# Mixture-of-experts products on Trainium2: 64-token stationaries split into 32-token column groups, and pairs for visits of three groups

## The chip, the cores and the metric

One core of one Trainium2 chip runs the whole kernel. The metric is the device time of one execution in microseconds (us); the figure compared is the median of several runs. A profiled execution has a span, measured by the hardware profiler, and a device time of its own a little above it. All data are float32.

## What is computed

One encoder layer: a mixer (attention and a state-space branch, about the first quarter of the time, not touched by the change), and then a mixture of experts over 512 tokens with 32 experts, four of which each token uses:

```python
logits = t @ w_router + b_router
top_val, top_idx = lax.top_k(logits, TOP_K)
top_w = softmax(top_val)
...
def expert_block(xb, e):
    g = xb @ w_gate[e] + b_gate[e]
    u = xb @ w_up[e] + b_up[e]
    g = minimum(g, 7.0)
    u = clip(u, -7.0, 7.0)
    act = g * sigmoid(1.702 * g) * (u + 1.0)
    return act @ w_down[e] + b_down[e]
...
out = zeros_like(t).at[row_tok].add(ys * row_w[:, None])
```

Each of `w_gate[e]`, `w_up[e]`, `w_down[e]` is 1024 x 1024 float32, 4 MB. The 96 matrices, some 400 MB, must all be read from memory once.

## The kernel before

**Positions, groups and visits.** Experts are ranked by their number of tokens, and processed one at a time at 32 positions. The table `RANK_GROUPS` (line 56) says how many groups of `TOK` = 32 tokens a rank gets, and `positions()` mixes large and small experts so that the work up to a position stays near `PACE` = 2.65 groups per position. The result, in order of position, is 3 3 2 3 2 3 3 2 3 3 2 3 2 3 2 2 4 2 2 4 2 2 4 2 2 2 5 2 1 5 1 1 groups, 82 in all. A position is served by one visit, a position of five groups by two, one of four groups and one of one. So there are 15 visits of two groups, 9 of three, 5 of four and 5 of one.

**The product.** For each visit and each of three matrices `product()` (line 1991) goes through eight blocks k of 128 rows of the matrix. The activations, transposed so that the contraction lies on the partitions, are the stationary operand; the weights stream. A group of 32 tokens that goes alone ("a single") has four matmuls for each k: the same 128x32 stationary is loaded in column group q = 0..3 of the array, and streams the q-th quarter of the weight's columns, 256 of them. Its result lies on 32 partitions for each quarter. Two groups that go together ("a pair") have two matmuls for each k: a 128x64 stationary in each half of the array, and each streams 512 columns. `pairs(vi)` and `singles(vi)` (lines 554 and 557) decide: a visit with an even number of groups is all pairs, one with an odd number all singles. `part_columns(vi)` (line 560) lists the parts with their columns in the accumulator. I call all matmuls of a part for one k a **round**. The trace has two records for each float32 matmul, so a round of a pair has four records and a round of a single has eight.

**The weights.** The weights come in 384 pieces of 1 MB (two blocks k each), issued by SyncE (SP) in the fixed order `STREAM` through a ring of `NRING` = 17 buffers. SP may issue the load of piece n only when the product that read piece n - 17 has released its buffer (`load` and `piece_used`, the issue itself is line 699). 17 pieces are there, or on their way, when the first product starts.

**Around the products.** PE's order is written out by hand (`stage` and the two tables of hooks in the block of TensorE): within the gate and up products of position j it makes the token lists of position j + 2 (line 1942, and `replicate`, line 1954), turns the tokens' rows of position j + 1 (line 1970) and turns the activations of position j - 1 (line 1983). VectorE (DVE) adds the bias to each product (`plus_bias`, the operation itself is recorded at line 1154), clamps and multiplies (lines 1518, 1532, 1534), and copies the expert's bias rows out to all groups (`biases`, a stream shuffle at line 1546). ScalarE (ACT) weighs the rows of the down product (line 1111). GpSimd (POOL) adds them to the output with accumulating indirect DMAs, one for each part (`scatter`, line 855): a single writes quarter rows of 1 KB, a pair half rows of 2 KB. It also gathers the tokens' rows (line 843). All DMAs of SP and POOL share 16 DMA engines.

Of the kernel before, what the change touches and what calls it, by code (L numbers as in the profile page):

```python
# [17 lines left out]
KT = DM // P  # L18
# [27 lines left out]
TOK = 32  # L46
# [44 lines left out]
VISITS, AT = visits()  # L91
NV = len(VISITS)
# [206 lines left out]
def hybrid_layer(nc, d, out, hn):  # L299
    ctx = ExitStack()  # L300
    with ctx:
# [28 lines left out]
        gm_c = const[:, C_GM:C_EPS]  # L330
# [87 lines left out]
        pieces = [cut(slots[n], KP, DE) for n in RING_AT]  # L418
# [130 lines left out]
        at_turn = {u: divmod(n, 2) for n, u in enumerate(TURNING)}  # L549
        at_unit = {u: divmod(n, SETS) for n, u in enumerate(UNITS)}  # L550
        at_piece = {u: divmod(n, NRING) for n, u in enumerate(STREAM)}
        scattered = [sum(g if (g := VISITS[w][1]) % 2 else g // 2 for w in range(v)) for v in range(NV + 1)]

        def pairs(vi):
            return 0 if vi.j is None or vi.G % 2 else vi.G // 2

        def singles(vi):
            return vi.G - 2 * pairs(vi)
# [584 lines left out]
        def _(dve):  # L1143
            v = nc.vector
# [321 lines left out]
            def index(vi):  # L1466

                c = spread(vi)
                use = vi.turns["d", 0]
                ps = wait_turned(dve, use)  # L1470
                at_least(dve, s_gath[vi.b], vi.gathers * 16)
                v.tensor_scalar(out=index_of(vi)[0:c, :].bitcast(I32), in0=ps[0:c, 0:1], scalar1=far_c[0:c, vi.G - 1:vi.G], scalar2=None,  # L1472
                                op0=ALU.add).then_inc(s_idx, 1)
                if pairs(vi) == 1 and not singles(vi):
                    ins = v.tensor_copy(dmask[vi.b][0:c, 0, :], ps[0:c, 0:2])
                else:
                    n = pairs(vi) + singles(vi)
                    blocks = {(0, 4): gm_c[:, 2:6], (2, 0): gm_c[:, 0:2], (0, 3): gm_c[:, 2:5],
                              (0, 1): gm_c[:, 2:3]}[pairs(vi), singles(vi)]
                    ins = v.tensor_tensor(out=dmask[vi.b][0:c, 0:n, :],  # L1480
                                          in0=ps[0:c, 0:2].unsqueeze(1).to_broadcast([c, n, 2]),
                                          in1=blocks[0:c, :].unsqueeze(2).to_broadcast([c, n, 2]), op=ALU.mult)
                ins.then_inc(s_tfree[use[1]], 1)
# [200 lines left out]
        def _(pe):  # L1684
# [301 lines left out]
            def product(vi, m, piece, first, last_visit, hooks=None):  # L1986
# [14 lines left out]
                for r in range(PIECES):  # L2001
                    pturn, slot = piece(m, r)
                    if first:
                        pe.wait_ge(s_raw[slot], 16 * (pturn + 1))
                    for kk in range(KP):
                        k = r * KP + kk
                        if hooks and k in hooks:
                            hooks[k]()
                        for n_, col, w in part_columns(vi):
                            t0, tn = col * TOK // QW, w * TOK // QW  # L2010
                            if m < 2:
                                x = xT[:, k, t0:t0 + tn]
                            else:
                                x = aT[n_][:, r % 2 * KP + kk, r // 2, :] if w == HW else aT[n_][:, kk, r, :]
                            for q in range(DM // w):
                                last = T.matmul(ps[q * tn:(q + 1) * tn, col:col + w], x,  # L2016
                                                pieces[slot][:, kk, q * w:(q + 1) * w],
                                                start=(k == 0 and col % 512 == 0), stop=(k == KT - 1),
                                                skip_group_check=True)
                    if last_visit and r < PIECES - 1:  # L2020
                        last.then_inc(s_used[slot], 1)
                last.then_inc(s_ufull[n], 1)
# [107 lines left out]
```

## Time and profile before

| | us |
|---|---|
| median of 3 runs | 1365.55 (1364.6 to 1369.87) |
| the profiled execution, its own time | 1366.18 |
| its span | 1364.3 |
| PE busy in the span | 1307.2 |
| DVE busy | 484.7 |
| ACT busy | 212.6 |
| POOL busy | 170.3 |

The expert products run from 353 us to 1358 us of the span. The profile records matmuls with modelled ends, so a matmul's mean duration contains the depth of the pipeline; the rate of a stream of matmuls is read from the time between the first starts of two neighbouring rows of the timeline, divided by the number of records. The share of a DMA queue is the time that its packets took, over 16 engines and the stretch.

### The profile page before, as it was taken

The numbers are of one execution on the slowest core, as the hardware profiler recorded it, in microseconds if no ns is written. First come the engines' busy times: TensorE is split into PE (matmuls) and PEld (weight loads), VectorE is DVE, ScalarE is ACT, GpSimd is POOL, SyncE is SP. The second block draws the span as 40 slices with busy tenths as digits, with TensorE's granted clock in tenths as the row PEclk, the third lists the DMA queues.
The fourth block names the chain that finished last, engine by engine and source line by source line (L and its number), as shares of the span: only waits on it lengthen the run. The fifth ranks groups of instructions, "written<-read, shape, count | busy, mean of one in ns | idle before, by whom it ended". The sixth has DMA issues, their size and how long they took to land.

```text
span 1364.3 us, 25613 instructions
## 1 busy us (share of the span) xinstructions
PE 1307.2 (96%) x10758; PEld 640.4 (47%) x10758; DVE 484.7 (36%) x1124; ACT 212.6 (16%) x461; POOL 170.3 (12%) x130
## 2 busy tenths in 40 slices
PE   8999989998899999999999998999999998999995
PEld 3465565655554555555464543333333333344342
DVE  1874576645332322222223322332322322232221
ACT  2132244332101110111100110111110001001010
POOL 0031220000201111110110111010010010011001
PEclk9989999998799999999999999999999999999998
DMA  9300420044999999999999999999999999999996
GB/s 372 124 1 0 166 100 1 33 184 170 349 342 394 406 414 397 418 399 412 407 410 415 408 416 406 416 413 410 417 406 418 417 405 417 414 414 397 410 415 229
DMA packets 77925, 448.28 MB, mean 329 GB/s; under 512 B 13080, under 2 KB 16392, under 8 KB 28656
## 3 DMA queue, kind: packets, MB, share of 16 engines
q1 hardware_dynamic: 63936, 426.51, 76.2%
q0 software_dynamic: 13296, 17.98, 5.5%
q8 instruction: 88, 1.44, 0.4%
q10 hardware_dynamic: 576, 2.10, 0.4%
q14 instruction: 29, 0.24, 0.0%
HBM read 442.61 MB, written 14.94 MB: 335 GB/s over the span
## 4 chain that ended last, share of the span: by engine, by line
PE 57%; SPq 29%; DVE 5%; DMA 5%; issue 2%; ACT 1%; POOL 1%; POOLq 0%; ACTq 0%; DVEq 0%
PE pair L2016 35%; SPq L699 28%; PE pair L1844 4%; PE pair L1745 4%; PE pair L1706 3%; DMA ring<-in_w_down 2%; DMA ring<-in_w_gate 2%; DVE rest L1154 2%; PE pair L1970 2%; PE pair L1701 2%; DVE rest L1185 1%; PE pair L1942 1%; PE pair L1983 1%; PE pair L1874 1%; PE pair L1834 1%
## 5 line engine op out<-in xcount | busy, mean ns | idle before, releaser
L2016 PE MATMUL pair<-ring,rest 128*32 128x256 f32 (+1 forms) x7952 | 832.8, 443 | 21.8 <-DMA ring<-in_w_down 14.9
L2016 PEld LDWEIGHTS pair<-ring,rest 128*32 128x32 f32 (+1 forms) x7952 | 332.4, 118 | 437.9 <-issue 288.2
L1154 DVE TENSOR_TENSOR rest<-pair,rest 128x512 f32<-128x512 f32 (+3 forms) x133 | 100.0, 755 | 426.4 <-PE pair L2016 399.0
L855 POOL DMA_INDIRECT out<-rest x57 | 89.6, 1572 | 745.1 <-ACT rest L1111 639.6
L1111 ACT ACTIVATE rest<-rest 128x256 f32<-128x256 f32 (+1 forms) x57 | 31.8, 596 | 513.6 <-DVE rest L1154 513.6
L1093 ACT ACTIVATE rest<-rest 128x512 f32<-128x512 f32 (+3 forms) x34 | 24.4, 718 | 303.4 <-DVE rest L1518 303.4
L1472 DVE TENSOR_SCALAR rest<-pair,rest 96x1 int32<-96x1 f32 (+2 forms) x34 | 7.3, 215 | 176.7 <-PE pair L1942 169.9
L1745 PE MATMUL pair<-ring 128*128 128x512 f32 (+1 forms) x192 | 69.6, 522 | 0.0
L1154 DVE TENSOR_TENSOR rest<-rest 128x512 f32<-128x512 f32 (+8 forms) x85 | 56.6, 678 | 32.1 <-ACT rest L1093 26.7
L1706 PE MATMUL pair<-ring 128*128 128x512 f32 x128 | 58.5, 617 | 5.6 <-DMA ring<-in_w_in 5.6
L2016 PE MATMUL pair<-rest 128*32 128x256 f32 (+1 forms) x592 | 62.1, 439 | 1.5 <-DMA rest<-in_w_down 1.5
L1546 DVE STREAM_SHUFFLE rest<-rest 128x512 f32<-128x512 f32 (+2 forms) x96 | 61.6, 642 | 0.0
L1844 PE MATMUL pair<-ring,rest 128*128 128x512 f32 x128 | 60.4, 621 | 0.9 <-DVE rest L1154 0.9
L843 POOL DMA_INDIRECT rest<-normed_rows,rest x34 | 35.9, 1056 | 161.7 <-DVE rest L1472 99.5
L1745 PEld LDWEIGHTS pair<-ring 128*128 128x128 f32 x192 | 36.6, 192 | 32.2 <-issue 30.7
L1970 PEld LDWEIGHTS pair<-rest 96*128 96x128 f32 (+2 forms) x272 | 35.4, 214 | 24.6 <-issue 24.6
L1970 PE MATMUL pair<-rest 96*128 96x96 f32 (+2 forms) x272 | 40.8, 293 | 3.4 <-DMA rest<-normed_rows,rest 2.7
L1706 PEld LDWEIGHTS pair<-ring 128*128 128x128 f32 x128 | 25.1, 198 | 37.3 <-issue 31.7
L1494 DVE TENSOR_SCALAR rest<-pair,rest 128x1 int32<-128x1 f32 (+2 forms) x34 | 7.5, 219 | 97.8 <-PE pair L1954 97.7
L1085 ACT ACTIVATE rest<-pair 128x256 f32<-128x256 f32 (+3 forms) x68 | 28.0, 428 | 74.6 <-PE pair L1970 73.3
L2016 PEld LDWEIGHTS pair<-rest 128*32 128x32 f32 (+1 forms) x592 | 23.7, 117 | 31.1 <-issue 17.9
L1844 PEld LDWEIGHTS pair<-ring,rest 128*128 128x128 f32 x128 | 24.2, 196 | 27.4 <-issue 26.2
(190 smaller groups left out, 860.4 us busy)
## 6 DMA issues: line engine op xcount, KB each, us to landing
ring<-in_w_gate SPq DMA_DIRECT2D x121, 1024.0 KB, 26.6
ring<-in_w_down SPq DMA_DIRECT2D x121, 1024.0 KB, 27.5
ring<-in_w_up SPq DMA_DIRECT2D x119, 1024.0 KB, 26.6
rest<-in_w_up SPq DMA_DIRECT2D x9, 1024.0 KB, 23.5
rest<-in_w_gate SPq DMA_DIRECT2D x7, 1024.0 KB, 26.5
rest<-in_w_down SPq DMA_DIRECT2D x7, 1024.0 KB, 28.1
ring<-in_w_in SPq DMA_DIRECT2D x8, 520.0 KB, 8.3
ring<-in_x SPq DMA_DIRECT2D x8, 512.0 KB, 13.0
```

What stands on the lines that cost most here:

```text
L699: sp.dma_start(pieces[slot], piece_source(m, e, r)).then_inc(s_raw[slot], 16)
L843: p.indirect_dma_start(out=hrow[vi.b][0:c, :], out_offset=None, in_=hn_d, in_offset=bass.IndirectOffsetOnAxis(ap=index_of(vi)[0:c, :].bitc ...
L855: p.indirect_dma_start(out=out_halves if w == HW else out_rows, out_offset=bass.IndirectOffsetOnAxis(ap=sidx[vi.ring][:, n:n + 1].bitcast( ...
L1085: nc.scalar.activation(rows_, src, ACT.Copy).then_inc(s_tfree[use[1]], 1)
L1111: ins = nc.scalar.activation(y, y, ACT.Copy, scale=wv[vi.ring][:, n:n + 1])
L1154: return v.tensor_tensor(out=out, in0=a, in1=b, op=op)
L1546: lk(v.stream_shuffle(out=bias_x[:, lo:hi], in_=btab[:, 3 * m * QW + lo:3 * m * QW + hi], mask=[j] * TOK))
L1706: return T.matmul(ps[:, :], w_in[:, k, XBC0 + ch * P:XBC0 + (ch + 1) * P], hTm[:, k, :], start=(k == 0), stop=(k == KT - 1))
L1745: last = T.matmul(ps[:, 0:b - a], src[:, k, t * P:(t + 1) * P], w[:, k, a:b], start=(k == 0), stop=(k == KT - 1))
L1844: last = T.matmul(ps[:, :], src[:, k, :], w[:, k, h * 512:h * 512 + 512], start=(k == 0), stop=(k == KT // 2 - 1))
L1970: last = T.transpose(ps[:, k * c:(k + 1) * c], kp_rows(hrow[vi.b][0:c, :], PIECES)[:, r, :, kk], ident[0:c, 0:c])
L2016: last = T.matmul(ps[q * tn:(q + 1) * tn, col:col + w], x, pieces[slot][:, kk, q * w:(q + 1) * w], start=(k == 0 and col % 512 == 0), stop ...
```

## The change

It does two things. In `product()` each matmul of a pair is cut in two along its tokens: a round of a pair is now four matmuls, each with a 128x32 stationary in one of four column groups, and each streams 512 columns as before; two of them stream the same half. And `pairs(vi)` is now G // 2 also for an odd G, so a visit of three groups is a pair and a single, and a visit of one stays a single. The number of scatters and the block masks follow. The overflow visits (experts with more tokens than their groups hold) keep their singles.

```diff
@@ block of positions and visits
-        scattered = [sum(g if (g := VISITS[w][1]) % 2 else g // 2 for w in range(v)) for v in range(NV + 1)]
+        scattered = [sum((VISITS[w][1] + 1) // 2 for w in range(v)) for v in range(NV + 1)]

         def pairs(vi):
-            return 0 if vi.j is None or vi.G % 2 else vi.G // 2
+            return 0 if vi.j is None else vi.G // 2
@@ index, on DVE
-                    blocks = {(0, 4): gm_c[:, 2:6], (2, 0): gm_c[:, 0:2], (0, 3): gm_c[:, 2:5],
+                    blocks = {(0, 4): gm_c[:, 2:6], (2, 0): gm_c[:, 0:2], (1, 1): gm_c[:, 0:5:4],
                               (0, 1): gm_c[:, 2:3]}[pairs(vi), singles(vi)]
@@ product, on PE
                             for q in range(DM // w):
-                                last = T.matmul(ps[q * tn:(q + 1) * tn, col:col + w], x,
-                                                pieces[slot][:, kk, q * w:(q + 1) * w],
-                                                start=(k == 0 and col % 512 == 0), stop=(k == KT - 1),
-                                                skip_group_check=True)
+                                for t in range(0, tn, TOK):
+                                    last = T.matmul(ps[q * tn + t:q * tn + t + TOK, col:col + w], x[:, t:t + TOK],
+                                                    pieces[slot][:, kk, q * w:(q + 1) * w],
+                                                    start=(k == 0 and col % 512 == 0), stop=(k == KT - 1),
+                                                    skip_group_check=True)
```

**How instructions move.** First PE, before, from the last rounds of the up product of position 1 (a visit of three, 32x256) through the gate product of position 2 (a visit of two, 64x512). The number after x counts matmuls of one kind in a row; `ring` and `rest` hold the weights and the activations, `pair` is the accumulator, and a width is that of the stationary, then the columns streamed.

```order
 L2016 MATMUL pair<-ring,rest 32x256 x120
 L2016 MATMUL pair<-ring,rest 64x512 x2
 L1983 MATMUL pair<-rest 128x128 x6
 L2016 MATMUL pair<-ring,rest 64x512 x2
 L2016 MATMUL pair<-rest 64x512 x4
 L2016 MATMUL pair<-ring,rest 64x512 x2
 L1942 MATMUL pair<-rest 96x2 x4
 L2016 MATMUL pair<-ring,rest 64x512 x12
 L1970 MATMUL pair<-rest 128x96 x8
```

The same place in the change:

```order
 L2017 MATMUL pair<-ring,rest 32x512 x4
 L2017 MATMUL pair<-ring,rest 32x256 x4
 L2017 MATMUL pair<-ring,rest 32x512 x4
 L1983 MATMUL pair<-rest 128x128 x6
 L2017 MATMUL pair<-ring,rest 32x512 x4
 L2017 MATMUL pair<-rest 32x512 x8
 L2017 MATMUL pair<-ring,rest 32x512 x4
 L1942 MATMUL pair<-rest 96x2 x4
 L2017 MATMUL pair<-ring,rest 32x512 x24
 L1970 MATMUL pair<-rest 128x96 x8
 L2017 MATMUL pair<-ring,rest 32x512 x12
 L1954 MATMUL pair<-rest 128x2
```

A visit of three now changes between four matmuls of 512 columns and four of 256 in each round. The visit of two has its hooks (lines 1983, 1942, 1970, 1954) after the same rounds, with twice as many matmuls between them.

DVE at position 0, around its up product, before (`places` of position 2, the bias add at line 1154, the clamp and the product with the gate, and the shuffle of the gate bias of the next position):

```order
 L1494 TENSOR_SCALAR rest<-pair,rest 128x1
 L1496 COPY rest<-pair 128x1
 L1154 TENSOR_TENSOR rest<-pair,rest 128x768
 L1532 TENSOR_SCALAR rest<-rest 128x768
 L1534 SCALAR_TENSOR_TENSOR rest<-rest 128x768
 L1546 STREAM_SHUFFLE rest<-rest 128x256
```

and in the change:

```order
 L1494 TENSOR_SCALAR rest<-pair,rest 128x1
 L1496 COPY rest<-pair 128x1
 L1154 TENSOR_TENSOR rest<-pair,rest 128x512
 L1154 TENSOR_TENSOR rest<-pair,rest 128x256
 L1532 TENSOR_SCALAR rest<-rest 128x768
 L1534 SCALAR_TENSOR_TENSOR rest<-rest 128x768
 L1546 STREAM_SHUFFLE rest<-rest 128x768
```

The bias add of the visit of three became two, one for the pair and one for the single, and the shuffle copies 768 columns where it copied 256.

POOL, the scatters of positions 0 and 1 between the gathers:

```order
 L843 DMA rest<-normed_rows,rest 128x1024 x3
-L855 DMA out<-rest 2048x256 x3
+L855 DMA out<-rest 1024x512
+L855 DMA out<-rest 2048x256
 L843 DMA rest<-normed_rows,rest 128x1024
```

Three scatters of quarter rows became one of half rows and one of quarter rows; nothing changed its place.

## Rows read from the trace of the kernel before

**Rows 1.** The page: DMA queues, their packets, MB, share of 16 engines.

```profile
q1 hardware_dynamic: 63936, 426.51, 76.2%
q8 instruction: 88, 1.44, 0.4%
```

**Rows 2.** Windows: busy us (x records) of each engine, PE clock, DMA share, GB/s.

```profile
353.00:400.00 47.00, 45.45 (x722) 27.38 (x726) 16.79 (x64) 5.66 (x10) 5.12 (x6) 0.97 0.94 353
400.00:500.00 100.00, 100.00 (x1236) 50.91 (x1232) 27.56 (x73) 10.13 (x21) 14.21 (x10) 1.00 1.02 399
500.00:600.00 100.00, 100.00 (x1422) 54.60 (x1418) 26.57 (x69) 11.19 (x24) 14.18 (x10) 1.00 1.02 409
1000.00:1100.00 100.00, 98.66 (x480) 36.19 (x478) 27.69 (x71) 9.88 (x17) 9.48 (x7) 1.00 1.02 413
```

**Rows 3.** DMA view, window 500 to 600: SP's queue; gate loads, us to landing.

```profile
q1 hardware_dynamic: 5336, 38.87, 93.7%
ring<-in_w_gate SPq DMA_DIRECT2D x12, 1024.0 KB, 18.6
```

**Rows 4.** The same views for 353 to 400 and 700 to 800.

```profile
q1 hardware_dynamic: 2025, 14.76, 82.7%
ring<-in_w_gate SPq DMA_DIRECT2D x3, 1024.0 KB, 6.5
...
ring<-in_w_gate SPq DMA_DIRECT2D x12, 1024.0 KB, 28.2
```

**Rows 5.** Chain that ended last, its end: start us, us, what.

```profile
1328.10 29.05 DMA ring<-in_w_down
1357.20 1.11 PE pair L2016 x16
```

**Rows 6.** Groups of PE by shape: xcount | busy us, mean ns | idle before.

```profile
L2016 PE MATMUL pair<-ring,rest 128*64 128x512 f32 x2256 | 509.4, 597 | 11.6 <-DMA ring<-in_w_down 6.4 <-DMA ring<-in_w_gate 3.6 <-DMA ring<-in_w_up 1.5
L2016 PE MATMUL pair<-ring,rest 128*32 128x256 f32 x5696 | 325.2, 382 | 10.2 <-DMA ring<-in_w_down 8.5 <-ACT rest L1103 1.1 <-issue 0.6
L1706 PE MATMUL pair<-ring 128*128 128x512 f32 x128 | 58.5, 617 | 5.6 <-DMA ring<-in_w_in 5.6
L1954 PE MATMUL pair<-rest 96*128 96x2 f32 x36 | 6.9, 262 | 0.0
```

**Rows 7.** PE's timeline, a visit of three: start us, us, what.

```profile
505.70 5.39 PE L2016 MATMUL pair<-ring,rest 128*32 128x256 f32 x96
511.02 0.84 PE L1942 MATMUL pair<-rest 128*96 128x2 f32 x8
```

**Rows 8.** PE's timeline, a visit of two.

```profile
729.41 5.37 PE L2016 MATMUL pair<-ring,rest 128*64 128x512 f32 x24
734.71 1.20 PE L1970 MATMUL pair<-rest 96*128 96x96 f32 x8
```

**Rows 9.** Line 2016's weight loads, 540 to 560: ns min/median/max.

```profile
L2016 PEld LDWEIGHTS pair<-ring,rest x276: 106/110/110, 540.1 to 560.0; 128*32 128x32 f32 x138
```

**Rows 10.** Queue of POOL in 572 to 580, then in 537 to 545.

```profile
q0 software_dynamic: 89, 0.09, 7.0%
...
q0 software_dynamic: 108, 0.20, 13.8%
```

**Rows 11.** Groups of DVE by shape, 420 to 1364.

```profile
L1546 DVE STREAM_SHUFFLE rest<-rest 128x256 f32<-128x256 f32 x31 | 13.8, 444 | 0.0
L1154 DVE TENSOR_TENSOR rest<-pair,rest 128x512 f32<-128x512 f32 x45 | 31.1, 692 | 132.1 <-PE pair L2016 132.1
L1154 DVE TENSOR_TENSOR rest<-pair,rest 128x768 f32<-128x768 f32 x22 | 21.1, 958 | 109.0 <-PE pair L2016 109.0
L1154 DVE TENSOR_TENSOR rest<-pair,rest 128x256 f32<-128x256 f32 x15 | 6.4, 425 | 40.5 <-PE pair L2016 40.4
L1546 DVE STREAM_SHUFFLE rest<-rest 128x768 f32<-128x768 f32 x6 | 6.1, 1019 | 0.0
```

**Rows 12.** PE's timeline at the turn of position 0's activations.

```profile
383.01 0.98 PE L1983 MATMUL pair<-rest 128*128 128x128 f32 x6 [1.38 <-DVE rest L1534]
```

## Prediction

> **What bounds the kernel now.** I read the page's queues first. SP's queue moved 426.5 MB and was busy for 76% of the whole span [rows 1]; nearly all of that is the 384 pieces of weights, which lie in the second three quarters. So the windows come next [rows 2]. PE looks full in each of them, but its ends are modelled, so that alone decides nothing. The DMA share is 1.02 in every window from 400 us on, at 409 to 413 GB/s, and below that only at the start: 0.94 at 353 GB/s from 353 to 400, 399 GB/s from 400 to 500. The DMA view tells why [rows 3, 4]. A piece landed 6.5 us after its issue at the start, after 18.6 us from 500 to 600, after 28.2 us from 700 to 800. SP issues a load when PE has released its buffer. With 38.87 MB in 100 us a piece of 1.05 MB takes 2.70 us of the engines, so 2 loads were on their way at the start, 7 later, 10 in the end. At the start PE's releases set the pace; from about 450 us on a queue stands before the DMA engines, and it grows: PE releases faster than they deliver. The end of the chain agrees: the last piece was issued at 1328.10, took 29.05 us, and only one piece's work and the last scatter follow it [rows 5].
>
> So the experts' phase is bound by the DMA engines except in its first 50 to 100 us. An edit counts if it takes work from the DMA engines, or lets PE release the first buffers sooner. PE's lead over DMA is small, though: the landing time grew by 9.6 us over 200 us, and a position of 12 pieces takes 12 x 2.70 = 32.4 us, so PE gains 1.55 us per position. A change that cost PE more than this would turn the bound round.
>
> **Term 1, the rounds of pairs.** I take the rates from the timeline. A single's round has 8 records: 96 records from 505.70 to 511.02 [rows 7] are 55.4 ns each, 443 ns for a group. A pair's round has 4 records: 24 from 729.41 to 734.71 [rows 8] are 220.8 ns each, 883 ns for two groups, 442 for one. The two forms cost the same per group. A full-width matmul of 512 columns takes 58.5 / 128 = 457 ns per record [rows 6]. The mean durations of 512 and 256 columns differ by 597 - 382 = 215 ns [rows 6], so streaming 512 columns takes some 430 ns in its column group. What is left per record is 457 - 430 = 27 ns for 128 tokens, 220.8 - 215 = 5.8 for 64, and 55.4 - 53.8 = 1.6 for 32.
>
> The new form, 32 tokens and 512 columns, is in no row. Its ideal is 430 / 4 = 107.5 ns per record. The nearest row by stationary and by number of groups is the single, so I take 107.5 + 1.6 = 109.1, a round of 8 records 873 ns. The ends are 107.5 (860 ns) and, with the remainder of the 64-token form, 113.3 (906 ns). Against 883 this saves 10 ns, or saves 23, or costs 23. For a visit of three the round goes from 3 x 443 = 1329 to 873 + 443 = 1316. A position has 24 rounds: -0.24 us for two groups, -0.31 for three. The visit of three also has a second small matmul pair for its index lists, 0.26 us (line 1954) [rows 6], which leaves -0.05. Where DMA is the bound this gives nothing. In the 3 or 4 positions before the queue stands it gives about **-0.4 us**, within -2 and +2 (four positions with the ends above).
>
> **Term 2, the scatters.** POOL's queue in 572 to 580, under the scatters of a visit of three, had 89 packets of 0.09 MB, thus of 1 KB: 7.0% of 8 us x 16 engines is 8.96 us, 101 ns each. In 537 to 545, under a visit of two, 108 packets of some 1.9 KB took 17.7 us, 164 ns each [rows 10]. Two packets of 1 KB that become one of 2 KB save 2 x 101 - 164 = 38 ns. A pair has 64 tokens, two half rows each: at most 128 merges per visit. The third group of a visit holds the expert's last tokens and often isn't full, and padding isn't written. The table of slots puts it in the pair, so between 64 and 128 merges happen. Nine visits: 576 to 1152 merges, 22 to 44 us of one engine, 1.4 to 2.7 us of sixteen. I take **-2.0 us**, in full, because the DMA engines are the bound there. The ends: nothing, if the freed time falls on engines that wait for others; and -7.3 us, if a 2 KB packet cost no more in the stream than a 1 KB one (1152 x 101 ns / 16).
>
> **Term 3, small costs.** DVE gets two bias adds for one, 692 + 425 - 958 = 0.16 us, three times per visit of three, and shuffles of 768 columns for 256, 1019 - 444 = 0.58 us, three times [rows 11]: 2.2 us per such position, 20 us in all. It is busy for 27 us in 100 [rows 2], and one position lasts 32, so it is hidden. The exception is the wait at 383.01, where PE stood 1.38 us for position 0's activations [rows 12]: this grows by **0.2 us**. The shuffle there is queued behind the operation that PE waits for. If DVE's cover went, 2.2 us would stand per position of three; nothing points there. Instructions are fetched by DMA too: 0.4% of the span, 5.5 us [rows 1]. The records of line 2016 go from 8544 to 9216, each with a weight load, 1344 more instructions on 25613, 5%: **+0.3 us**.
>
> POOL issues two scatters for three; ACT two weighings for three: neither is waited for.
>
> **The sum.** -0.4 - 2.0 + 0.2 + 0.3 = -1.9 us, against the profiled execution's 1366.2 us: 1364.3. That execution lies 0.6 above the median of the runs shown, so on the median's scale it is **1363.6 us**. A measurement of this kernel can tell about 0.5% from no change, 6.8 us: I forecast no change that can be told.
>
> **Rival A: slower, the extra weight loads don't hide.** A round of a pair has eight weight loads where it had four. Mechanism: a load into a column group waits for that group's running matmul, and adds its 110 ns [rows 9] to each of the group's two records in a round: 2 x (430 + 110) = 1080 ns for 883, or 1523 for 1329 with a single. That is 4.7 us more per position of two or three groups and 9.5 for four. The first 17 positions (nine of three, seven of two, one of four) need 16 x 4.7 + 9.5 = 85 us more, of which PE's lead takes 17 x 1.55 = 26: +58, at least 1424 us. It decides from 1.55 us per position on, that is 65 ns per round, a record of 119 ns for my 109. Against it: in the single's round eight loads of 110 ns, 880 ns, already lie within 443 ns [rows 7, 9]. The Trainium skill's page "TensorE: Matmul & The Clock Gate", Part 3, says that a weight load overlaps matmuls in flight only where their row groups differ. All four stationaries here use the same rows, so by it this rival would come true. By that rule the trace disagrees for 256 columns; for 512 no row speaks. I give A a chance of 0.09, with values from +7 up.
>
> **Rival B: faster, the DMA engines gain more.** The scatter's lower end, -7.3, with -2 at the start and +0.5 of costs: -8.8, 1356.8 us. For it: windows with many small packets also move less on SP's queue (409 GB/s against 413 in all). Against it: two thirds of the bytes stay as they are. Chance 0.13 for a gain over 6.8 us. A perfect PE could not give much more by itself: at the rate of 38.9 MB per 100 us the window 353 to 400 missed 18.3 - 14.8 = 3.5 MB [rows 3, 4], 9 us.
>
> **Rival C: nothing moves.** Engines that idle for others swallow the merged packets, and the new rounds come out at 906 ns: 0 for term 2, +2 for term 1, +0.5 for term 3, together +2.5, 1368 us. A pair form slower by 23 ns costs 0.6 us per position, which PE's lead of 1.55 still covers. Chance 0.25.
>
> **How the numbers follow.** Forecast (-5 to 0) 0.53, C 0.25, B 0.13, A 0.09. Faster by over 0.5%: B, 0.13. Slower: A, with a little from C's far end, 0.10. Within: 0.77. The range must leave out at most 0.2: it leaves out nearly all of A and part of B, and runs from 1357 (B's value) to 1369 (C's, with a microsecond for the runs).
>
> **What would show it.** In the timeline, 32-token rounds of 512 columns at 109 ns per record; 115 or more speaks for C, over 119 for A. Landing times at 700 to 800 us still near 28 us, the DMA share 1.02: right. Landing times that fall below 15 us there, with gaps of the DMA share: A. POOL's queue with some 600 to 1100 fewer data packets. PE's wait for position 0's activations at 1.5 us. I am wrong if the span moves by more than 7 us while the bytes and DMA share per window stay.

## The result, and the profile after

The median went from 1365.62 to 1368.43 us (20 runs each). The ratio is 1.0025, interval 1.0017 to 1.0034: **3.4 us slower**, where I had forecast 1.9 us faster. The medians as they stand differ by 2.8 us; one of the 20 executions of the kernel before took 2228.47 us, and the ratios here and below are taken without such executions. The time lies within my range, but the sign is wrong. The profiled execution took 1369.9 us, its span 1367.8 (before 1366.18 and 1364.3).

The page of the changed kernel, its DMA queues; they answer to [rows 1]:

```profile
q1 hardware_dynamic: 63936, 426.51, 76.1%
q0 software_dynamic: 12000, 17.98, 5.4%
q8 instruction: 93, 1.52, 0.4%
```

The weights' queue is as it was. POOL's (q0) lost 1296 packets (it had 13296, 5.5%), with the same bytes. The instruction queue has five packets more, 93 for 88. The windows, in the columns of [rows 2]:

```profile
353.00:400.00 47.00, 45.55 (x461) 19.92 (x456) 16.83 (x61) 3.72 (x7) 4.99 (x5) 0.89 0.84 315
400.00:500.00 100.00, 100.00 (x1066) 40.54 (x1062) 34.02 (x89) 11.12 (x22) 11.10 (x8) 1.00 1.02 401
500.00:600.00 100.00, 100.00 (x1118) 41.37 (x1114) 29.35 (x75) 9.98 (x19) 11.07 (x8) 1.00 1.02 410
1000.00:1100.00 100.00, 97.40 (x874) 32.72 (x870) 27.84 (x71) 9.88 (x17) 9.49 (x7) 1.00 1.02 413
```

From 400 us on they answer to those of before: the DMA share is 1.02. The first is different: 315 GB/s for 353, and a granted clock of 0.89 for 0.97. The DMA view of the changed kernel, for 353 to 400, 500 to 600 and 700 to 800 (queue: packets, MB, share; loads: count, KB, us to landing), against [rows 3, 4]:

```profile
q1 hardware_dynamic: 1814, 13.16, 74.4%
...
q1 hardware_dynamic: 5368, 39.08, 94.0%
q0 software_dynamic: 1152, 1.82, 7.6%
ring<-in_w_gate SPq DMA_DIRECT2D x14, 1024.0 KB, 15.9
...
ring<-in_w_gate SPq DMA_DIRECT2D x12, 1024.0 KB, 31.4
```

1.60 MB are missing at the start, 4.0 us at the 39.9 MB per 100 us that the queue moved later (800 to 900). From 500 to 600 0.21 MB more moved than before, with POOL's queue at 7.6% for 8.0. Now the rounds. PE's timeline (start, us, what), first a visit of three, then one of two:

```profile
387.88 5.37 PE L2017 MATMUL pair<-ring,rest 128*32 128x512 f32 x64
393.17 0.84 PE L1942 MATMUL pair<-rest 128*96 128x2 f32 x8
...
731.95 5.36 PE L2017 MATMUL pair<-ring,rest 128*32 128x512 f32 x48
737.24 1.20 PE L1970 MATMUL pair<-rest 96*128 96x96 f32 x8
```

A round of a pair takes (737.24 - 731.95) / 6 = 882 ns, 110.2 per record, for 883 before [rows 8]. Four rounds of a visit of three take 5.29 us, 1322 ns each for 1329 [rows 7]. The new form is neither faster nor slower. Its weight loads hide.

The start of the first product, on PE's timeline: before, and in the change.

```profile
353.17 2.77 PE L2016 MATMUL pair<-ring,rest 128*32 128x256 f32 x24 [0.63 <-issue]
355.87 0.39 PE L1954 MATMUL pair<-rest 96*128 96x6 f32 x2
356.18 1.50 PE L2016 MATMUL pair<-ring,rest 128*32 128x256 f32 x24
```

```profile
352.56 2.79 PE L2017 MATMUL pair<-ring,rest 128*32 128x512 f32 x16 [0.63 <-issue]
355.28 1.01 PE L1954 MATMUL pair<-rest 96*128 96x2 f32 x4
356.22 2.79 PE L2017 MATMUL pair<-ring,rest 128*32 128x512 f32 x16
358.94 1.44 PE L1942 MATMUL pair<-rest 128*96 128x2 f32 x8
360.31 2.79 PE L2017 MATMUL pair<-ring,rest 128*32 128x512 f32 x16
```

The product's rows (L2016, L2017) are one round each. At 1.2 GHz it takes 2.8 us, at 2.4 GHz 1.5 with its ends; before, only the first is slow, in the change all three are. Windows of 2 us show the clock (the last column but two), first before, then in the change:

```profile
354.00:356.00 2.00, 2.00 (x21) 0.80 (x14) 0.00 (x0) 0.37 (x1) 1.45 (x2) 0.55 1.02 410
356.00:358.00 2.00, 2.00 (x31) 1.23 (x31) 0.29 (x2) 0.00 (x0) 0.00 (x0) 1.00 0.98 397
```

```profile
360.00:362.00 2.00, 2.00 (x11) 0.69 (x14) 0.78 (x5) 0.00 (x0) 0.59 (x1) 0.50 1.01 315
362.00:364.00 2.00, 2.00 (x20) 1.15 (x16) 0.43 (x3) 0.00 (x0) 0.41 (x1) 0.55 0.88 305
364.00:366.00 2.00, 2.00 (x24) 0.73 (x28) 1.75 (x11) 0.00 (x0) 0.00 (x0) 1.00 0.23 88
```

In both kernels PE had waited with little work, its clock at 0.50, until this product began. Before, the clock was up 3 us after the start of the product; in the change, 11 us. PE is 3.8 us behind at the end of the first gate product (its turn begins at 372.71, before at 368.95), and the DMA share falls to 0.23, since SP waits for releases. PE's wait for position 0's activations is 1.45 us, for 1.38 [rows 12]:

```profile
386.96 0.99 PE L1983 MATMUL pair<-rest 128*128 128x128 f32 x6 [1.45 <-DVE rest L1534]
```

The chain's end, against [rows 5] (issue, us, what): the last piece is issued 2.4 us later, and the last matmuls begin 2.3 us later.

```profile
1330.54 28.89 DMA ring<-in_w_down
1359.47 1.11 PE pair L2017 x16
```

### The profile page after: what moved, and what is told of

Read it like the earlier page. It is cut to its first block, busy times and chain, and to the rows that moved or that the text cites. A ratio compares the mean times of both kernels' runs of the same rounds, so it can differ in the third digit from the quotient of the medians.

```text
span 1367.8 us, 27002 instructions
## 1 busy us (share of the span) xinstructions
PE 1307.8 (96%) x11448; PEld 572.3 (42%) x11448; DVE 503.8 (37%) x1160; ACT 211.1 (15%) x452; POOL 156.5 (11%) x121
## 4 chain that ended last, share of the span: by engine, by line
PE 59%; SPq 26%; DVE 5%; DMA 5%; issue 2%; ACT 1%; POOL 1%; POOLq 0%; ACTq 0%; DVEq 0%
PE pair L2017 38%; SPq L699 26%; PE pair L1844 4%; PE pair L1745 4%; PE pair L1706 3%; DMA ring<-in_w_down 2%; DMA ring<-in_w_gate 2%; DVE rest L1154 2%; PE pair L1970 2%; PE pair L1701 1%; DVE rest L1185 1%; PE pair L1942 1%; PE pair L1983 1%; PE pair L1874 1%; PE pair L1834 1%
## 5 line engine op out<-in xcount | busy, mean ns | idle before, releaser
L2017 PE MATMUL pair<-ring,rest 128*32 128x512 f32 (+1 forms) x8608 | 832.9, 536 | 22.3 <-DMA ring<-in_w_down 13.1
L2017 PEld LDWEIGHTS pair<-ring,rest 128*32 128x32 f32 x8608 | 267.2, 110 | 500.7 <-issue 416.1
L1154 DVE TENSOR_TENSOR rest<-pair,rest 128x512 f32<-128x512 f32 (+2 forms) x160 | 101.8, 653 | 420.1 <-PE pair L2017 381.0
L855 POOL DMA_INDIRECT out<-rest x48 | 75.6, 1575 | 748.3 <-ACT rest L1111 643.6
L1111 ACT ACTIVATE rest<-rest 128x512 f32<-128x512 f32 (+1 forms) x48 | 30.2, 656 | 515.4 <-DVE rest L1154 515.4
L1546 DVE STREAM_SHUFFLE rest<-rest 128x512 f32<-128x512 f32 (+2 forms) x96 | 77.8, 810 | 0.0
L2017 PE MATMUL pair<-rest 128*32 128x512 f32 (+1 forms) x608 | 62.0, 533 | 1.1 <-DMA rest<-in_w_down 1.1
L1494 DVE TENSOR_SCALAR rest<-pair,rest 128x1 int32<-128x1 f32 (+1 forms) x43 | 8.5, 216 | 93.1 <-PE pair L1954 93.0
L1353 DVE TENSOR_SCALAR rest<-rest 128x96 f32<-128x96 f32 (+2 forms) x136 | 27.9, 269 | 25.4 <-PE pair L1970 17.8
L1942 PEld LDWEIGHTS pair<-rest 128*96 128x96 f32 (+2 forms) x272 | 27.1, 171 | 23.2 <-issue 23.1
```

The costliest lines, as they stand in the source:

```text
L855: p.indirect_dma_start(out=out_halves if w == HW else out_rows, out_offset=bass.IndirectOffsetOnAxis(ap=sidx[vi.ring][:, n:n + 1].bitcast( ...
L1111: ins = nc.scalar.activation(y, y, ACT.Copy, scale=wv[vi.ring][:, n:n + 1])
L1154: return v.tensor_tensor(out=out, in0=a, in1=b, op=op)
L1546: lk(v.stream_shuffle(out=bias_x[:, lo:hi], in_=btab[:, 3 * m * QW + lo:3 * m * QW + hi], mask=[j] * TOK))
L1942: last = T.matmul(ps[0:c, 0:2], buf[:, t, :], pay[vi.b][:, t, :], start=(t == 0), stop=(t == NT - 1))
L2017: last = T.matmul(ps[q * tn + t:q * tn + t + TOK, col:col + w], x[:, t:t + TOK], pieces[slot][:, kk, q * w:(q + 1) * w], start=(k == 0 and ...
```

## The experiments

Three accounts stood after this: the late clock, the split of the even visits' pairs, and the pairs in visits of three. In the diffs `tn` is the number of tokens of a part. All kernels below compute the same output.

**The split alone.** The kernel before, with this loop; visits of three and one as before:

```diff
-    last = T.matmul(ps[q * tn:(q + 1) * tn, col:col + w], x,
+    for t in range(0, tn, TOK):
+        last = T.matmul(ps[q * tn + t:q * tn + t + TOK, col:col + w], x[:, t:t + TOK],
```

> Only the first half of the change: pairs of two- and four-group visits as four 32-token matmuls of 512 columns; visits of three stay singles, as before. Theory T (the late clock: the first products, at position 0, now run for 7 us longer at the granted clock 0.5, PE is 4 us late and the DMA engines starve meanwhile): position 0 is again as before, so the clock rises near 356 us, DMA moves about 14.8 MB on SP's queue from 353 to 400, and the time is that of before: ratio 0.999 to 1.001. Rival R (the 32-token form of pairs reads the weights from memory on chip twice as often and slows the DMA engines or PE all through the products): the slowdown is here in full, ratio 1.002 to 1.003.

1368.38 us, 1.0024 [1.0012, 1.0036] against 1364.94. The clock was up at 355.2 us (before: 355.8), but the first product had begun at 350.39, so it rose 4.8 us after this, for 2.6 before; in the change it was 11.2. So the split alone can cost as much as the whole change, without a clock as late as that. The same kernel later, beside another group of runs:

> The same kernel as in the first group of runs (even visits' pairs split along their tokens at every position, visits of three as before), again, for comparison on the same chip as the two others: 1.0024 within 0.0012 of before, 119.4 MB on SP's queue from 800 to 1100. If it comes out within 0.001 of before, the cost of the split depends on the chip or the program's placing and the first result was not a property of the split.

1368.48 us, 1.0025 [1.0014, 1.0036]; it repeats. In this profile the clock rose 5.7 us after the first product's start.

**Visits of three alone**, with a pair 64 tokens wide and a single in each round (the change without its inner loop):

```diff
-    for t in range(0, tn, TOK):
-        last = T.matmul(ps[q * tn + t:q * tn + t + TOK, col:col + w], x[:, t:t + TOK],
+    last = T.matmul(ps[q * tn:(q + 1) * tn, col:col + w], x,
```

> Only the second half: visits of three are a pair and a single, but a pair keeps its two 64-token matmuls of 512 columns. Theory T: what matters is when the clock rises at position 0. If the mix of 512-column pairs with singles is what delays it, it rises near 363 us here too and the ratio is 1.001 to 1.003; if it is the four-way 512-column form, it rises near 356, and the merged scatters show alone: ratio 0.998 to 0.999. Rival R: 0.998 to 0.999 with either clock. A third theory (the second bias add, the wider shuffles and the second index matmul of visits of three cost the time) wants 1.002 or more here with the clock rising at 356.

1400.59 us, 1.0264 [1.0241, 1.0286]. PE's timeline:

```profile
566.90 4.80 PE L2016 MATMUL pair<-ring,rest 128*64 128x512 f32 x36
571.64 3.23 PE L2016 MATMUL pair<-rest 128*64 128x512 f32 x24
```

A round now has 12 records, so 36 are three rounds in 4.74 us: 1580 ns for 1329. That is 6.0 us per visit of three, 54 us in nine; the kernel lost 36, so PE's lead took a part. The landing time from 500 to 600 fell to 6.5 us: here PE is the bound. The test doesn't isolate what I wanted, for it adds a cost that the change doesn't have: stationaries 64 and 32 wide in turn. One thing it does show: the clock rose 3.2 us after the first product's start, so 512-column pairs between singles don't delay it by themselves. The Trainium skill's "TensorEngine Tiling (Array Packing)", Key Properties, says that changing the tiling mode drains the engine; the trace fits this, with an estimated 125 ns per change ((1580 - 1329) / 2).

**The late clock, two ways.** The change with position 0 left in singles:

```diff
-            return 0 if vi.j is None else vi.G // 2
+            return 0 if vi.j is None or (vi.G % 2 and vi.n < 1) else vi.G // 2
```

> The changed kernel, but the visit of position 0 alone keeps its three singles. Theory T: the clock rises near 356 us as before, SP's queue moves about 14.8 MB from 353 to 400, and the slowdown is gone; the merged scatters of eight visits are left: ratio 0.998 to 0.9995. Rival R and the third theory: 1.002 to 1.003, unchanged, since only one position of 32 differs.

The clock was up at 354.8 us, and SP's queue moved 14.46 MB from 353 to 400, 0.3 less than expected. The last matmuls began at 1355.30, 1.9 us sooner than before. Yet the time is 1370.79, 1.0044 [1.0028, 1.0060]. The end of each engine's program tells why (ns min/median/max, when):

```profile
L301 SPq COMPARE_BRANCH  x1: 38/38/38, 1364.3 to 1364.3; - x1
L301 SPq DRAIN  x1: 7/7/7, 1364.4 to 1364.4; - x1
L301 PEldq DRAIN  x1: 8/8/8, 1368.5 to 1368.5; - x1
```

SP saw the work done at 1364.3, but PE reached its end 4.2 us later; before, PE's came 0.4 us after SP's. Two more runs went after this. One put 128 instructions that never run into PE's last, skipped block:

```diff
+                for _ in range(128):
+                    pe.sem_inc(s_pad, 1)
                 dispatch(vi)
```

> The kernel with singles at position 0, once more, with 128 instructions that never run in PE's overflow body, which PE jumps over at the end. In that kernel's profile PE reached the end 4.2 us after SP had seen the last scatter, with two fetches of instructions in that time. Theory P (where the end of PE's program falls in its blocks of instructions decides how long the jump takes): PE's last drain comes within 0.5 us of SP's, and the ratio falls from 1.0044 to 1.0005 to 1.002. If the 4 us are something else of that kernel, it stays at 1.004.

1371.82, 1.0036 [1.0017, 1.0054]; PE's end came 7.7 us after SP's, where theory P wanted 0.5 at most. The other put the same two lines at the start of PE's program instead, where they run:

> The kernel with singles at position 0, with 128 semaphore increments at the start of PE's program, in the 5.6 us in which it waits for the first load: all of PE's code lies half a block of 16 KB later, the jump at the end too. Theory P (the block in which the jump starts decides): PE's last drain comes within 0.5 us of SP's and the ratio is 1.000 to 1.002, for 1.0044 unshifted. Otherwise 1.003 to 1.0055, and the late end of PE is open.

1.0111 [1.0091, 1.0131]: the increments delayed the first product by over 10 us, so its time says nothing. PE's end did come ahead of SP's. The place of PE's program in its fetches may matter at the end, but of its two tests one failed and one is spoiled; the late end stays open.

The other way warms the array: three matmuls whose result nobody reads, in the wait before the first product, in the change and in the kernel before.

```diff
+            for _ in range(3):
+                T.matmul(bank[5][:, 0:256], ones, const[:, C_ID:C_SLOT], start=True, stop=True)
             turn_rows(v0)
```

> The changed kernel with three matmuls of 256 columns whose result nobody reads, in the 2.5 us in which PE waits for the first gather (at 348 us). Theory T: PE is busy through this wait, the clock rises before 356 us or so, the first products run at clock 1.0, and the time falls by 3 to 6 us: ratio to before 0.997 to 1.000. Rival R: nothing changes after position 0, at most a microsecond is gained: 1.0015 to 1.003.

> The kernel before with the same three unread matmuls in PE's wait for the first gather. In its own profile the clock rose near 356 us, so the late clock can cost it 3 us of the first products at most. Theory L (late clock as one of several terms): the clock rises 2 to 4 us sooner after the first product's start, ratio 0.998 to 1.000. If the gain of the same edit in the changed kernel (2.4 us) had nothing to do with the clock, it should be the same here: 0.998 in any case, with the clock where it was.

With them the change takes 1365.99, 1.0011 [0.9994, 1.0028], and the kernel before 0.9994 [0.9984, 1.0004]. The clock was full before the product began:

```profile
354.08 1.50 PE L2017 MATMUL pair<-ring,rest 128*32 128x512 f32 x16 [0.63 <-issue]
```

and 14.78 MB moved from 353 to 400. By the ratios (1.0025 and 1.0011) 1.9 us came back, with some 2.6 us on either side, for the two intervals overlap. The profiles show more. From the first product's start to the turn of position 0's activations PE needed 29.2 us, in the change without the three matmuls 34.4. After the turn the two kernels are alike:

```profile
383.25 0.98 PE L1983 MATMUL pair<-rest 128*128 128x128 f32 x6 [1.44 <-DVE rest L1534]
1355.83 1.11 PE pair L2017 x16
```

**Are instruction fetches the cost of the split?** It doubles the matmuls of pairs: 30413 instructions for 25613, 106 packets of the instruction queue for 88. Two runs added fetches to the kernel before by increments of a semaphore on an engine that is seldom waited for: 150 per position on POOL (`s_moves`), and 13 ahead of each load on SP.

```diff
                     for vi in visit_at[j - 1]:
                         scatter(vi)
+                    for _ in range(150):
+                        pool.sem_inc(s_moves, 1)
```

```diff
                 if turn:
+                    for _ in range(13):
+                        sp.sem_inc(s_pad, 1)
                     piece_used(sp, n - NRING)
```

> The kernel before with 150 semaphore increments more on POOL per position, 4950 instructions of no effect, about as many as the pairs' split adds on PE when it is made alone (4800). Theory F (fetching more instructions takes DMA time from the weights): the page's queue 8 rises from 88 to some 105 packets, SP's queue moves 0.2 to 0.3% less from 800 to 1100 us, ratio 1.0008 to 1.002. If instead the split itself is what slows the DMA engines (four streams read the weights where two did): 0.9995 to 1.0005.

> The kernel before with 13 semaphore increments on SP ahead of the wait of each of its 367 loads from the ring's second turn on: 4771 instructions of no effect, as many as the split of the pairs alone adds on PE, but on an engine that mostly waits. (The same number on POOL made the scatters late by 8 us, so that run did not test this.) Theory F (the fetches themselves take the DMA time): packets of the instruction queues up by 15 to 40, SP's queue moves 0.2 to 0.3% less from 800 to 1100 us, ratio 1.0008 to 1.002. If the four streams of the new pair are the cause: 0.9995 to 1.0005 and 119.6 to 119.7 MB in that stretch.

1.0208 [1.0189, 1.0227] and 1.0119 [1.0100, 1.0137]. The 88 packets of queue 8 stayed 88. The fetches came in the other instruction queue, q14, with 66 packets for 29, of 8 KB where queue 8 has 16 KB. And both runs brought far more than fetches: POOL's gathers came 6 to 8 us late from 480 to 560 (491.14 for 483.09 us) and its last scatter 19 us late, and SP's queue lost most from 1100 to 1300. The instructions weren't free, so neither run tells the theories apart.

**The split in one half.** From position 16 on, then up to 15, in the kernel before:

```diff
+    tw = TOK if vi.G % 2 or (vi.j is not None and vi.j >= 16) else tn
```

> The kernel before with its pairs split only from position 16 on: 19 of the 25 pairs, all where the DMA engines are the bound, none where PE sets the pace. Theories F and R agree on the place and want three quarters of the 3.4 us that the whole split costs, 1.5 to 3 us: ratio 1.001 to 1.002, and 119.3 to 119.4 MB on SP's queue from 800 to 1100. If the cost comes from the start, where PE paces the loads, it is gone: 0.9995 to 1.0005.

> The kernel before, with the pairs of the even visits split along their tokens only at positions 0 to 15 (seven visits of two groups); from position 16 on they stay 64 tokens wide. Together with the run that split only from position 16 (1.0004, interval 0.9989 to 1.0018) this should add up to the split everywhere (1.0024). If the cost sits in the early positions: 1.001 to 1.0025, with SP's queue 0.1 to 0.6 MB below before between 353 and 800 us, and 119.7 MB from 800 to 1100. If it sits in the DMA-bound second half: 1.000 within 0.001.

1.0004 [0.9989, 1.0018] for the late half and 1.0006 [0.9994, 1.0018] for the early one. Neither can be told from nothing; their sum, 1.0010 with some 0.0019 on either side, holds the whole's 1.0024. By these times the place of the cost is open. The profile of the late half, which splits 18 of the 25 pairs (not 19), has the missing bytes: 119.42 MB from 800 to 1100 for 119.67, with 21 instruction packets for 13.

**Instructions without the four streams.** The pairs keep 64 tokens and two column groups; each matmul is cut along its columns instead:

```diff
-    for q in range(DM // w):
-        last = T.matmul(ps[q * tn:(q + 1) * tn, col:col + w], x,
+    for h, q in ((h, q) for h in range(0, w, 256) for q in range(DM // w)):
+        last = T.matmul(ps[q * tn:(q + 1) * tn, col + h:col + h + 256], x,
```

> The kernel before, with each matmul of a pair (visits of two and four groups) cut in two along its columns instead of its tokens: 128x64 stationaries in two column groups, 256 columns streamed, two column groups at work as before, and as many matmuls, weight loads and instructions as in the kernel that splits only the even visits' pairs (some 30400 instructions for 25613, some 18 more instruction fetches). Theory F (the cost of the split is the instruction stream: more fetches on the shared DMA engines): 1.002 to 1.003 of before, 7 instruction packets per 100 us from 800 to 1100 and 119.4 MB on SP's queue there, as in the kernel with the split. Theory S (the cost is four column groups reading four streams, or the split along the tokens): 1.000 within 0.0012, and 119.7 MB there. If a round of a pair takes much more than 883 ns (over 950), weight loads of 64 columns hide worse with short streams, the test says little, and the time goes above 1.005.

1.0018 [1.0003, 1.0033]. The round (eight records; six rounds):

```profile
728.96 5.40 PE L2016 MATMUL pair<-ring,rest 128*64 128x256 f32 x48
734.29 1.19 PE L1970 MATMUL pair<-rest 96*128 96x96 f32 x8
```

888 ns for 883, well within PE's lead. The DMA view of 800 to 900, in order: before, this kernel, the split alone, and the split up to position 15 (four answers).

```profile
q1 hardware_dynamic: 5480, 39.94, 95.8%
q8 instruction: 5, 0.08, 0.3%
```

```profile
q1 hardware_dynamic: 5471, 39.86, 95.7%
q8 instruction: 7, 0.11, 0.5%
```

```profile
q1 hardware_dynamic: 5476, 39.86, 95.7%
q8 instruction: 7, 0.11, 0.5%
```

```profile
q1 hardware_dynamic: 5483, 39.91, 95.8%
q8 instruction: 6, 0.10, 0.4%
```

Over 800 to 1100 the weights' queue moved 119.67 MB before, 119.33 here and 119.32 with the split, with 13, 21 and 21 instruction packets. In the kernel split only up to position 15, 119.62 MB and 14. So the loss of bytes goes with the number of instructions and needs neither four streams nor 32-token stationaries. For the time the same is likely: the interval of 1.0018 holds 1.0024 and excludes 1. That the fetches' traffic is what each instruction costs is argued from these bytes; no run changed the fetches and nothing else.

**A version without either cost.** Pairs of even visits 64 wide as before, the pair in a visit of three split into 32s; first with the three warming matmuls, then without:

```diff
+    tw = TOK if vi.G % 2 else tn
+    for t in range(0, tn, tw):
```

> A version that takes only what the terms say pays: visits of three as a 32-token pair and a single (merged scatters, fewer matmuls), visits of two and four with the two 64-token matmuls of before, and the three unread matmuls ahead of the first product. Sum by the terms: scatters -1.9 us, some 14 fetches of instructions fewer -0.9, no more four-stream pairs from 800 us on, clock at least as early as before, a tail of 0 to 1.2 us: 1362.5 to 1364, ratio 0.997 to 0.999. If the pair of the visits of three is what costs the time: 1.001 or more.

> The version with a 32-token pair and a single for visits of three and 64-token pairs for the others, without the three unread matmuls. Late-clock theory: the clock rises 6 to 10 us after the first product's start, as in the changed kernel, and the 2 to 2.5 us that the three matmuls saved there are lost here too: ratio 0.9985 to 1.000 against 0.998 with them. If the clock doesn't matter: 0.998.

**1362.77 us, 0.9980 [0.9971, 0.9989]**, and 1363.67, 0.9981 [0.9969, 0.9993]. Both beat both kernels. They have 22213 and 22202 instructions and 74 instruction packets, and moved 119.7 MB from 800 to 1100. The profile of the second has the late clock (up 10.8 us after its first product's start, 13.12 MB from 353 to 400), though by the two ratios it costs nothing, within 2 us.

```profile
350.06 2.79 PE L2018 MATMUL pair<-ring,rest 128*32 128x512 f32 x16 [0.63 <-issue]
384.26 0.98 PE L1983 MATMUL pair<-rest 128*128 128x128 f32 x6 [1.44 <-DVE rest L1534]
1354.87 1.11 PE pair L2018 x16
```

**The profiled executions in stretches.** Three times cut each of them up in the same way: the start of the first product, the turn of position 0's activations (line 1983), and the start of the last 16 matmul records in the chain. For the split alone the last two are:

```profile
381.20 0.99 PE L1983 MATMUL pair<-rest 128*128 128x128 f32 x6 [1.38 <-DVE rest L1534]
1357.37 1.11 PE pair L2017 x16
```

All numbers are in us; "clock" is how long after the first product's start the clock was up, from windows of 2 us.

| kernel | first product | clock | position 0 | from there to the last matmuls | to the end of the span |
|---|---|---|---|---|---|
| before | 353.17 | 2.6 | 29.84 | 974.19 | 7.10 |
| before, warmed | 354.14 | before it | 28.90 | 974.34 | 6.92 |
| the change | 352.56 | 11.2 | 34.40 | 972.51 | 8.33 |
| the change, warmed | 354.08 | before it | 29.17 | 972.58 | 8.27 |
| split alone | 350.39 | 4.8 | 30.81 | 976.17 | 8.23 |
| split alone, again | 353.87 | 5.7 | 31.24 | 976.05 | 7.14 |
| split from position 16 | 353.35 | 3.9 | 30.36 | 975.81 | 8.08 |
| split up to position 15 | 353.86 | 3.5 | 30.19 | 974.46 | 8.59 |
| halved columns | 351.69 | 3.9 | 30.36 | 975.50 | 7.25 |
| mixed, warmed | 350.26 | before it | 29.22 | 970.26 | 8.36 |
| mixed | 350.06 | 10.8 | 34.20 | 970.61 | 8.13 |
| position 0 in singles | 349.98 | 4.8 | 31.04 | 974.28 | 13.50 |

Three things can be read from it. First, position 0 gets longer by about 0.5 us for each microsecond that the clock comes later, whatever the kernel. Second, the long stretch behind it depends on the kernel and not on the clock: kernels that differ only in the warming, or in nothing, agree within 0.4 us. The two other kernels with singles at position 0 agree as well, with 974.50 for the padded one (974.28 without the padding) and 974.30 for the one whose first product was 12 us late. Third, against the kernel before this stretch is 1.7 us shorter in the change, 1.9 to 2.0 longer with the split alone, 1.3 with halved columns, 1.6 and 0.3 with the two half splits, and 3.6 to 3.9 shorter in the mixed version. The last column differs by 1.1 us between two executions of one kernel.

So the change's own profile adds up: -0.6 for its earlier start, +4.6 at position 0, -1.7 behind it and +1.2 at the end are the 3.5 us of its span. Each row is one execution, however, and the unprofiled ones say less. For the mixed version they speak against a cost of 5 us: the ratio is 0.9981 without the warming and 0.9980 with it. The unwarmed one's profiled execution, 1365.0 us with a mean granted clock of 0.978, was one of the slower (the median clock of its executions is 0.980, that of the kernel before beside it too, and 0.9775 in the change). How late the clock was in the others was not recorded.

## Why the prediction was wrong

**The bound** was read rightly: the DMA share is 1.02 from 400 us on, the landing time at 700 to 800 us is 31.4 us, and the last piece decides.

**Term 1, the rounds: right in size, and the step that failed.** A record takes 110.2 ns for my 109.1, and the weight loads hide. But the term priced the first positions by rounds at the full clock and put the time until the clock rises at nothing. It forecast -0.05 us for position 0; the profile shows +4.6 (34.40 for 29.84). The clock was at 1.2 GHz for its first 11.2 us, before for 2.6, and half a microsecond for each of the 8.6 between is an estimated 4.3. The three warming matmuls took this away again in the profile (29.17); by the ratios they are worth 1.9 us, with 2.6 on either side. What makes the clock rise late was not tried further. Both unwarmed profiles with 32-token rounds of 512 columns at position 0 have it at about 11 us; with rounds of 256 columns there it is between 2.5 and 5.7, and this differs from execution to execution.

**Term 3, the instruction fetches: right in kind, too small per instruction.** I priced them by their packets' own time and got +0.3. The split alone adds 18 packets. From 500 to 600, 11 packets take 0.7% of 16 engines, 1.0 us each, so 18 own 1.1 us of the sixteen. The stretch behind position 0 grew by 1.9 to 2.0 us with them (by 1.3 with halved columns), about 0.1 us per packet; the whole time by 3.3 to 3.6 us, of which 1.0 to 1.4 is a longer position 0 under a clock that rose later. I also counted only the net growth of 5%. The visits of three fetch less than before and those of two and four nearly twice as much, and the latter fill the second half: 22 packets for 13 from 800 to 1100, and 119.40 MB for 119.67, 0.7 us at 39.9 MB per 100 us. By bytes a packet more costs 0.08 us in the change and 0.11 with the split alone (0.35 MB, 8 packets), against its own 0.06. At 0.11 us the change's five packets are +0.5 us.

**Term 2, the scatters: as forecast, as far as the profiles go.** 1296 packets went, nine times 144, where my upper end was nine times 128 merges. The queue's counts in most windows of 100 us are multiples of 144 (1440 three times before, with 1.87, 1.82 and 1.59 MB, then 1728, 1152 and 1008). So a scatter seems to be 144 packets whether its groups are full or not, and my reading that padding makes no packets was wrong. POOL's share fell by 0.4 points from 500 to 600 and by 0.4 from 700 to 800. Behind position 0 the change is 1.7 us shorter in spite of its five packets, which leaves -2.2 for the scatters. The mixed version is 3.6 to 3.9 shorter with 14 packets fewer (-1.5), which leaves -2.1 to -2.4. I forecast -2.0. This is a fit, not a test: no run had the merged scatters alone, and the kernel with singles at position 0 (nine packets more, eight ninths of the merges) should be 1.0 us shorter by it and is 0.1 to 0.3 longer. The ratios give less than the profiles: -2.7 us for the warmed mixed version, where position 0 and the stretch behind it give -4.5, and +2.3 for the warmed change against the warmed kernel before, where they give -1.5.

So for the stretch in which the DMA engines are the bound, terms 2 and 3 gave -1.7 us, and -1.7 was measured in the profile; that it fits so closely is in part luck, for both sizes are rough. By the change's profile the sign was lost at position 0.

**DVE's wait** grew by 0.07 us, not 0.2.

**The rivals.** A, loads that don't hide, is refuted: 882 ns. The Trainium skill's sentence in "TensorE: Matmul & The Clock Gate", Part 3, by which all of them would stand in the open, is contradicted by this row for 512 columns too; the same part also lets loads into a background weight buffer go ahead, and the trace doesn't speak against that. B didn't come. C gave 1368, and the time agrees, but by luck: its rounds of 906 ns didn't come, and by the stretches above the scatters' freed time was not swallowed.

**Open:** what delays the clock, how often it is late in executions that were not profiled (by the ratios the warming is worth 1.9 us in the change and nothing in the mixed version, by the profiles over 5 in both), and what the merged scatters are worth when nothing else changes.

## What to carry to other kernels

A new form of a loop has to be priced where it runs first, too, with the clock that it finds there: here 4.6 us of one position outweighed what the change saved in all the others. In a kernel bound by its DMA engines, count instructions as traffic. Doubling the matmuls of 20 of the 34 visits cost 0.2%, although each round took as long as before; a version with 13% fewer instructions and merged scatters gained as much. Of two forms that are equal in time, take the one with fewer instructions; and an experiment that adds "free" instructions must show that they are free. When medians can't tell two causes apart, cut the profiles into stretches at the same events.

## What was not expected of the hardware

- Stationaries 64 and 32 wide in turn within a round: 1580 ns for 1329, and 2.6% of the kernel. In separate visits they mix freely (1362.77 us).
- The clock's rise from 0.50 to 1.00 came 2.5 to 5.7 us after the first product's start with 256-column rounds (even one kernel's two profiles differ, 4.8 and 5.7), 3.2 with 64-token matmuls of 512 columns between singles, and about 11 with 32-token ones (11.2 and 10.8), all after a sparse stretch. Three matmuls of 256 columns in the wait before had it at 1.00 before the product began.
- PE's program ended 4.2 and 7.7 us after SP had seen all work done in two kernels, and ahead of SP's in others: time that no chain of work shows.
